# Gates by head in row halves, segment sums in float32r, the gelu eviction ahead of the mix and the norm total on VectorE, in a one-core hybrid decoder layer

## The reference, cut to what matters

```
def rg_lru(x, h0, gate_a_w, gate_a_b, gate_x_w, gate_x_b, lam):
    xb = xf.reshape(B, L, LRU_HEADS, LRU_BS)                  # 16 heads of 64
    r  = sigmoid(einsum('blhi,hij->blhj', xb, gate_a_w) + gate_a_b)
    ig = sigmoid(einsum('blhi,hij->blhj', xb, gate_x_w) + gate_x_b)
    log_a = -LRU_C * r * softplus(-lam)
    a = exp(log_a)
    u = sqrt(-expm1(2.0 * log_a)) * (ig * xf)
    _, h = associative_scan(_lin_combine, (a, u), axis=1)     # h = a*h + u
lru_out = rmsnorm(h * gelu(lru_y), lru_out_norm)

def ssd_scan(x, dt, A, Bm, Cm, h0):
    Acs = cumsum(dtc * A, axis=2)
    seg = Acs[:, :, :, None] - Acs[:, :, None, :]             # per head, 128 x 128 of a chunk
    Lmat = exp(where(causal, seg, -inf))
    y_diag = einsum('bcijg,bcijge,bcjgep->bcigep', CB, Lmat, xdt)
```

## Time and profile before

| what | value |
|---|---|
| median of 3 runs | 2287.48 us (2287.12 to 2287.72) |
| profiled execution, its own time | 2286.77 us |
| its span, first to last instruction | 2285.0 us |
| busy PE / DVE / POOL / ACT | 99% / 45% / 33% / 20% |
| one slot, in slots 2 to 7 | 40.2 us, of 2285 |
| mean granted PE clock | 0.997 |

### The profile page before, as it was taken

One profiled execution on the slowest core, in us unless ns is written; L12 is line 12 of the kernel. 1 busy time (PEld: TensorE's weight loads), 2 busy tenths in 40 slices (PEclk: granted clock), 3 DMA queues, 4 the chain that ended last, 5 costly groups with the idle time before them and its releaser, 6 DMA issues.

```text
span 2285.0 us, 31977 instructions
## 1 busy us (share of the span) xinstructions
PE 2254.6 (99%) x14337; PEld 2196.3 (96%) x14337; DVE 1021.3 (45%) x795; ACT 450.2 (20%) x561; POOL 758.2 (33%) x420
## 2 busy tenths in 40 slices
PE   8999999999999999999999999999999999999997
PEld 8999999999999999988888999999999999999997
DVE  6422122311233557867778586773231123212336
ACT  4100000000002225454453540120000001000102
POOL 4333333333333223333534642323333333333340
PEclk9999999999999999999999999999999999999999
DMA  4111111111112422310110422111111111111112
GB/s 150 47 47 47 47 47 46 47 47 47 47 42 79 129 75 93 119 46 31 52 40 32 175 75 87 47 47 47 47 47 47 47 47 47 47 47 47 47 56 75
DMA packets 48456, 138.87 MB, mean 61 GB/s; under 512 B 7608, under 2 KB 16312, under 8 KB 48320
## 3 DMA queue, kind: packets, MB, share of 16 engines
q1 hardware_dynamic: 47168, 135.78, 18.8%
q10 hardware_dynamic: 1152, 1.05, 0.1%
HBM read 118.19 MB, written 18.79 MB: 60 GB/s over the span
## 4 chain that ended last, share of the span: by engine, by line
PE 89%; DVE 6%; DVEq 2%; issue 1%; ACT 1%; DMA 1%; SPq 0%; ACTq 0%
PE set L568 82%; PE set L799 2%; DVEq L1321 1%; DVE lru_conv L1187 1%; PE pair L701 1%; PE set L701 1%; PE pair L709 1%; DVEq L1285 0%; DVE xbc L1291 0%; DVE e L1286 0%; PE set L588 0%; DVE power L1324 0%; DVEq L1289 0%; PE set L734 0%; PE set L731 0%
## 5 line engine op out<-in xcount | busy, mean ns | idle before, releaser
L457 POOL TENSOR_SCALAR w_hi<-w_raw 128x1024 fp32r<-128x1024 f32 (+1 forms) x181 | 193.9, 1071 | 1418.6 <-PE set L568 1228.5
L459 POOL TENSOR_TENSOR w_lo<-w_raw,w_hi 128x1024 fp32r<-128x1024 f32 (+1 forms) x181 | 445.2, 2460 | 27.6 <-issue 1.4
L568 PE MATMUL set<-x_lo,w_hi 128*128 128x344 f32 x2112 | 448.7, 321 | 3.5 <-DVE x_lo L1087 3.5
L568 PE MATMUL set<-x_hi,w_hi 128*128 128x344 f32 x2112 | 448.9, 321 | 0.8 <-ACT x_hi L842 0.8
L568 PE MATMUL set<-x_hi,w_lo 128*128 128x344 f32 x2112 | 446.2, 320 | 0.0
L568 PEld LDWEIGHTS set<-x_lo,w_hi 128*128 128x128 f32 x2112 | 357.3, 189 | 4.6 <-DVE x_lo L1087 4.6
L568 PEld LDWEIGHTS set<-x_hi,w_hi 128*128 128x128 f32 x2112 | 355.5, 188 | 1.4 <-issue 0.9
L568 PEld LDWEIGHTS set<-x_hi,w_lo 128*128 128x128 f32 x2112 | 352.0, 188 | 0.0
L1083 DVE TENSOR_TENSOR up<-set,rstd 128x1032 f32<-128x1032 f32 x43 | 53.0, 1233 | 419.8 <-PE set L568 419.8
L568 PE MATMUL set<-u_hi,w_hi 128*128 128x344 f32 x864 | 199.4, 339 | 8.5 <-DVE gelu L1083 5.5
L568 PE MATMUL set<-h_hi,w_hi 128*128 128x344 f32 x948 | 201.3, 321 | 0.8 <-DVE h_lo L1107 0.8
(11 more groups left out here) (252 smaller groups left out, 2601.2 us busy)
## 6 DMA issues: line engine op xcount, KB each, us to landing
w_raw<-in_gate_up SPq DMA_DIRECT2D x87, 512.0 KB, 3.5
w_raw<-in_w_in SPq DMA_DIRECT2D x36, 512.0 KB, 4.2
w_raw<-in_down SPq DMA_DIRECT2D x32, 512.0 KB, 3.5
w_raw<-in_w_out SPq DMA_DIRECT2D x16, 512.0 KB, 3.8
w_raw<-in_down SPq DMA_DIRECT2D x16, 384.0 KB, 3.2
x<-in_xt SPq DMA_DIRECT2D x8, 516.0 KB, 8.0
x_kept<-x SPq DMA_DIRECT2D x8, 516.0 KB, 5.0
mixed<-power SPq DMA_DIRECT2D x8, 516.0 KB, 2.9
```

Of the source, the lines that this page charges most:

```text
L457: pool.tensor_scalar(w_hi[s][:, 0:n], w_raw[s][:, 0:n], 1.0, 0.0, ALU.mult, ALU.add)
L459: pool.tensor_tensor(w_lo[s][:, 0:n], w_raw[s][:, 0:n], w_hi[s][:, 0:n].bitcast(F32), ALU.subtract).then_inc(split, 1)
L568: end = pe.matmul(out[:, c, 0:CH], w[s][:, k * P:(k + 1) * P], x[:, kx, c * CH:(c + 1) * CH], start=(first and n == 0), stop=(last and n = ...
```

## The change

It does the following, all of it in the slots but for two small conversions:

- **Gates.** The weights of a tile were two 128x128 block-diagonal matrices (one for each gate, two heads in each). Now they are one 128x128 array: rows 0 to 63 hold the first head's weights for gates a and x side by side, rows 64 to 127 the second head's, x first. `gate` issues six products with 64 rows of contraction, alternating between the row halves, into `pair` (second head) and `set1` (first head). ACT's sigmoids become four of 64 partitions x 1024 and four of 64x8.
- **Segment sums.** `a_tok` is split into a float32r high and low part (`a_hi`, `a_lo`, in the space of `dtw`); POOL makes one 128x2048 product of the high part and two of 128x1024 of the low part (`segr_lo`, which share memory with `lmat`); PE makes each segment sum as two accumulated float32r products in place of one float32 product.
- **Eviction and mix.** `gelu` and the LRU input share two buffers by parity; DVE evicts ly right behind the scan and mixes after it. The scan's result goes to `decay`, the 9-column copy moves to ACT, ACT's `lru_square` moves from the end of a slot to behind the gates of the next.
- **Norm total.** Tiles 1 to 5 of the LRU norm's total are added on DVE, ahead of `lru_power` (in slots 3 to 7), not on POOL.
- **High part of the lx weights.** ACT copies it (for `c` = 1 to 7), and POOL makes the low part alone.

```
@@ gpsimd
-                pool.wait_ge(landed[s], 16 * (u // 2 + 1))
-                pool.tensor_scalar(w_hi[s][:, 0:n], w_raw[s][:, 0:n], 1.0, 0.0, ALU.mult, ALU.add)
-                pool.drain()
+                if name[0] == "lx" and name[1]:
+                    pool.wait_ge(lx_high, name[1])
+                else:
+                    pool.wait_ge(landed[s], 16 * (u // 2 + 1))
+                    pool.tensor_scalar(w_hi[s][:, 0:n], w_raw[s][:, 0:n], 1.0, 0.0, ALU.mult, ALU.add)
+                    pool.drain()
                 pool.tensor_tensor(w_lo[s][:, 0:n], w_raw[s][:, 0:n], w_hi[s][:, 0:n].bitcast(F32),
                                    ALU.subtract).then_inc(split, 1)
...
             def seg_terms(c):
                 if c:
                     pool.wait_ge(seg_done, 2 * c)
+                    pool.wait_ge(y_done, 2 * c)
...
                 pool.tensor_tensor(segr[:], tri[:].unsqueeze(1).broadcast_to([P, HEADS, QC]),
-                                   a_tok[:, c, :].unsqueeze(2).broadcast_to([P, HEADS, QC]), ALU.mult).then_inc(segr_ready, 1)
+                                   a_hi[:, c, :].bitcast(F32).unsqueeze(2).broadcast_to([P, HEADS, QC]), ALU.mult)
+                for g in range(GROUPS):
+                    mine = a_lo[:, c, g * GH:(g + 1) * GH].bitcast(F32)
+                    pool.tensor_tensor(segr_lo[g][:], tri[:].unsqueeze(1).broadcast_to([P, GH, QC]),
+                                       mine.unsqueeze(2).broadcast_to([P, GH, QC]), ALU.mult).then_inc(segr_ready, 1)
...
-                if c >= 3:
-                    total("lru", c - 2, tl)
@@ tensor
                     for n in range(2):
-                        h = g * GH + 4 * n
-                        end = pe.matmul((set1 if g else pair)[:, n, :], later[:],
-                                        segr[:, h:h + 4, :].rearrange("p h t -> p (h t)"), start=True, stop=True)
+                        for low, part in enumerate((segr[:, g * GH + 4 * n:g * GH + 4 * n + 4, :],
+                                                    segr_lo[g][:, 4 * n:4 * n + 4, :])):
+                            end = pe.matmul((set1 if g else pair)[:, n, :], later_r[:],
+                                            part.rearrange("p h t -> p (h t)"), start=(low == 0), stop=(low == 1))
...
-                    for n in range(2):
-                        pe.matmul(set1[:, 2, n * DEC:(n + 1) * DEC], w[:, n, :], lacc[:, PROMPT:T],
-                                  start=True, stop=True)
-                    for n, out in enumerate((set1, pair)):
-                        for k in range(2):
-                            end = pe.matmul(out[:, k, :], w[:, n, :], lacc[:, k * 512:(k + 1) * 512], start=True, stop=True)
-                        end.then_inc(gate_products, 1)
+                    h0, h1 = slice(0, HD), slice(HD, P)
+                    pe.matmul(set1[:, 2, 0:DEC], w[h0, :], lacc[h0, PROMPT:T], start=True, stop=True).then_inc(gate_small, 1)
+                    for k in range(2):
+                        tokens = slice(k * 512, (k + 1) * 512)
+                        pe.matmul(pair[:, k, :], w[h1, :], lacc[h1, tokens], start=True, stop=True)
+                        end = pe.matmul(set1[:, k, :], w[h0, :], lacc[h0, tokens], start=True, stop=True)
+                    end.then_inc(gate_products, 1)
+                    pe.wait_ge(gate_small, c + 1)
+                    pe.matmul(set1[:, 2, DEC:2 * DEC], w[h1, :], lacc[h1, PROMPT:T],
+                              start=True, stop=True).then_inc(gate_products, 1)
@@ scalar
                 if c:
                     lru_gates(c - 1)
+                    if c > 1:
+                        lru_square(c - 2)
                     lru_decays(c - 1)
...
-                first_tap(XT + c, lraw, lacc)
-                if c:
-                    lru_square(c - 1)
+                first_tap(XT + c, lraw[c % 2], lacc)
+                if c < NCH - 1:
+                    u = U(("lx", c + 1))
+                    act.wait_ge(used, u - 1)
+                    act.wait_ge(landed[u % 2], 16 * (u // 2 + 1))
+                    act.activation(w_hi[u % 2][:], w_raw[u % 2][:], ACT.Copy).then_inc(lx_high, 1)
@@ vector
+                if c >= 3:
+                    lru_total(c - 2)
                 if c:
                     lru_power(c - 1)
                 mask(c, 0)
...
                 if c:
                     lru_scan(c - 1)
-                    dve.wait_ge(mixed_ready, c)
-                else:
-                    dve.wait_ge(state_stored[0], 32)
-                scaled(("ly", c), gelu[:], rstd)
+                dve.wait_ge(tails, XT + c + 1)
+                scaled(("ly", c), gelu[c % 2][:], rstd)
+                if c:
+                    lru_mix(c - 1)
```

More of the change, by code:

```diff
@@ L229, in build @@
         c_dec = [at(f"c_dec{g}", Y + k, [DEC, P]) for g, k in enumerate((6, 10))]
-        segr = at("seg_terms", Y, [HEADS, QC])
+        segr = at("seg_terms", Y, [HEADS, QC], F32R)
+        segr_lo = [at(f"seg_low{g}", Y + 2 + g, [GH, QC], F32R) for g in range(GROUPS)]
         lmat = [at(f"lmat{g}", Y + 2 + g, [GH, QC]) for g in range(GROUPS)]
@@ L237, in build @@
         cb = at("cb", Y + 8, [GROUPS, QC], skip=256)
-        gates = at("gates", Y + 8, [2, P], skip=512)
-        gates2 = at("gates2", Y + 8, [2, P], skip=768)
+        gates = at("gates", Y + 8, [P], skip=512)
+        gates2 = at("gates2", Y + 8, [P], skip=768)
         gate_a, gate_x, decay = (at(n, Y + 9 + k, [T]) for k, n in enumerate(("gate_a", "gate_x", "decay")))
-        lraw, lacc = at("lru_in", Y + 12, [T]), at("lru_conv", Y + 13, [T])
-        gelu, sq, sqn, tl = (at(n, Y + 14 + k, [T]) for k, n in enumerate(("gelu", "power", "square", "total_lru")))
+        lraw = gelu = [at("lru_even", Y + 12, [T]), at("lru_odd", Y + 14, [T])]
+        lacc = at("lru_conv", Y + 13, [T])
+        sq, sqn, tl = (at(n, Y + 15 + k, [T]) for k, n in enumerate(("power", "square", "total_lru")))
         zt, t0, t1 = (at(n, XB + k, [T]) for k, n in enumerate(("silu_z", "total_s0", "total_s1")))
@@ L922, in lru_gates, with sigmoid @@
                 par = pars[:, XT + t, :]
[L923 to L927 removed]
+                h0, h1 = slice(0, HD), slice(HD, P)
+                def sigmoid(to, source, at_rows, bias):
+                    return act.activation(to, source, ACT.Sigmoid, bias=par[at_rows, bias:bias + 1])
+                act.wait_ge(gate_products, 2 * t + 1)
+                sigmoid(halves(gate_a[h0, 0:PROMPT]), set1[h0, 0:2, :], h0, PAR_GA)
+                if t:
+                    act.wait_ge(scanned, t)
+                sigmoid(halves(gate_x[h0, 0:PROMPT]), set1[h1, 0:2, :], h1, PAR_GX)
+                act.wait_ge(gate_products, 2 * t + 2)
+                for to, rows, at_rows, cols, bias in ((gate_a, h0, h0, 0, PAR_GA), (gate_x, h0, h1, 0, PAR_GX),
+                                                      (gate_a, h1, h1, DEC, PAR_GA), (gate_x, h1, h0, DEC, PAR_GX)):
+                    last = sigmoid(to[rows, PROMPT:T], set1[at_rows, 2, cols:cols + DEC], at_rows, bias)
+                last.then_inc(gate_read, 1)
+                for to, at_rows, bias in ((gate_a, h1, PAR_GA), (gate_x, h0, PAR_GX)):
+                    last = sigmoid(halves(to[h1, 0:PROMPT]), pair[at_rows, 0:2, :], at_rows, bias)
+                last.then_inc(gate_read, 1)
             def lru_decays(t):
@@ L944, in lru_finish @@
                 freed(("ly", t))
-                act.activation(gelu[:], gelu[:], ACT.Gelu_apprx_tanh).then_inc(gelu_done, 1)
+                act.activation(gelu[t % 2][:], gelu[t % 2][:], ACT.Gelu_apprx_tanh).then_inc(gelu_done, 1)
             def lru_square(t):
@@ L954, in lru_square @@
                     act.wait_ge(added["lru"], t - 1)
+                act.activation(lru_h[:, t, :], decay[:, PROMPT - 1:T], ACT.Copy)
                 act.activation(sqn[:] if t else tl[:], sq[:], ACT.Square).then_inc(squared["lru"], 1)
@@ L1154, in prepare @@
                         dve.drain()
+                dve.wait_ge(consts, 1)
+                dve.tensor_copy(later_r[:], later[:])
                 dve.wait_ge(dtw_landed, 16)
```

59 lines of the change are left out of this document (35 added, 24 removed).

## The result

The changed kernel takes 2311.1 us (median; 2307.26 to 2314.32), the kernel before 2287.6 on the same chip: 1.0104 times, 95% interval 1.0092 to 1.0117, slower by 1.0%. The forecast was 2290.3 with a range to 2301, so the time lies 10 us outside it. The profiled execution, the fastest of the four, took 2307.26 us for a span of 2305.3, 20.3 longer than the span of 2285.0 before; 2.8 of it were forecast.

A forecast was written before the change was run, and what follows sets the result against it. PE, busy 99% of the span, was taken to bound the kernel. Slots 3 to 6 +6.5, slot 7 +1.2, slot 2 -1.1, slot 1 -2.2, slot 0 -1.6: +2.8 on the median 2287.48 gives 2290.3 us, range 2277 to 2301.

The forecast's parts named there:

- that the clock stays at full: All slots: PE keeps full clock despite five holes of 4 us, so no time was added for them.
- the rival of a falling clock: At `outputs(0)` in five slots: half clock behind PE's holes adds 2.8 each, 14 us, to 2304; chance 0.09.
- The main part of the forecast: The whole kernel: +2.8 us to 2290.3, with PE idle some 4 us ahead of `outputs(0)`; chance 0.50.
- Low products at 1.9: POOL in the slots: each new low product of the segment sums takes 1.9 us, 2.4 kept for the range.
- rival 3: POOL in slots 1 to 7: low products cost 2.4 us each like w_lo, +7 us, to 2297.3; chance 0.19.
- Part A: Steady slot from start of lx to start of `outputs(0)`: 21.1 us instead of 18.3, lost 2.8.
- The order at the port: DVE and POOL share a port, whoever asked first goes first: total, skip product, power product, the last ending at 15.3.
- Rival 1: DVE's power product gets in ahead of POOL's skip product: part A 1.7 us shorter in five slots, 2281.8; chance 0.14.
- Part B: Steady slot from `outputs(0)` to the next lx: 20.7 us through w_lo, scan and eviction, against 21.9; saved 1.2.
- Slots 0 and 1: First two slots: -1.6 us in slot 0 from `seg` and gate less waits, -2.2 in slot 1.
- Slot 7 and the z units: Last slot and behind: +2.8, less 1.3 for the gate and 0.3 at the first z unit, +1.2 us.
- the 17-pass pattern: Gates on PE: as in `widen`, second passes overlap the next product's first, 5 passes of 0.43, 2.1 us.

The follow-up runs named there:

- e2: The changed kernel with DVE's addition to the norm total moved behind the second mask; 2298.1 us, ratio 1.0052.
- e3: The changed kernel with twenty unread float32r products on PE ahead of L745 in slots 2 to 7; 2299.4 us, ratio 1.0055.
- e14: The changed kernel with total behind second mask, turn after set1's sigmoids, z load ahead, lmat[1] exp before root and gelu, lx high part on POOL; 2283.4 us.
- e7: The changed kernel with float32 segment sums, total behind second mask, turn waiting only for set1's sigmoids, z load ahead of the store; 2276.8 us.
- e1: The changed kernel with segment sums in float32 again, without low products on POOL; 2288.0 us, ratio 1.0009.
- e13: The changed kernel with ACT's exp of lmat[1] ahead of root and gelu, and DVE's gate product with the root behind the second mask; 2282.7 us.
- e6: The changed kernel with the load of z unit 3 issued ahead of the store of slot 7's mixed tile; 2304.0 us, ratio 1.0074.
- e11: The kernel before with only the eviction of ly ahead of the mix (and the moves it needs) and the z unit's load first; 2275.4 us.
- e8: The changed kernel with float32 segment sums, gates as before the change, total behind second mask, z load ahead of the store; 2276.3 us.
- e4: The changed kernel with gates as before the change: four products of 128 rows, four sigmoids; 2301.0 us, ratio 1.0065.

## Why the prediction was wrong, step by step

The spans, turn to turn, against the forecast's parts (which were cut at lx, some 5 us earlier):

| stretch | before | after | change | forecast |
|---|---|---|---|---|
| to the turn of slot 0 | 942.7 | 945.4 | +2.8 | 0 |
| slot 0 | 35.7 | 37.7 | +2.0 | -1.6 |
| slot 1 | 40.2 | 39.0 | -1.2 | -2.2 |
| slot 2 | 40.2 | 41.9 | +1.7 | -1.1 |
| slots 3 to 6 | 161.2 | 172.9 | +11.7 | +6.5 |
| last turn to the end | 1065.0 | 1068.3 | +3.3 | +1.2 |
| sum | 2285.0 | 2305.3 | +20.3 | +2.8 |

- **The step that failed: that the clock stays at full, with the rival of a falling clock at a chance of 0.09.** The main part of the forecast said itself that PE would stand idle some 4 us in five slots, and took no price for it. The runs give it: 0.8 to 1.6 us for a stretch of 3.4 us (e2, e3, e14) and 2.7 for the one of 6.8. Filling six of the holes took the ratio from 1.0104 to 1.0055 (e3), 11 us; on the forecast's base that is 2300, just inside its range. Nine stretches were seen in the change, which at these prices make some 9 to 16 of the missing 17.5 us (an estimate: those of the first slots were not filled by themselves). The rival was priced at 2.8 per hole in five slots. The rest is the waits at L702 in slots 0 and 1, slot 2's order and the z unit's load, below. The Trainium skill (TensorE: Matmul & The Clock Gate, Why this matters for your kernels) warns of idle gaps between bursts; here the trace agrees, at 0.50 behind holes of 2.1 to 4.0 us, though not behind every hole of 2.5 (e2).
- **The evidence against it was misread.** The prediction cited "in every slice" at full clock. A slice of the page is 57 us and a stretch 3.4, so the tenths could not show it. The windows of the kernel before do show one, and no hole of more than 0.25 us stands ahead of it, but 54 small products (most of 8 columns) in the two microseconds before:

```profile
840.00:842.00 2.00, 2.00 (x54) 1.98 (x52) 0.61 (x2) 1.47 (x3) 0.00 (x0) 1.00 1.11 260
842.00:846.00 4.00, 4.00 (x18) 4.00 (x17) 3.80 (x4) 1.17 (x2) 0.00 (x0) 0.57 0.62 189
846.00:848.00 2.00, 2.00 (x15) 2.00 (x14) 0.21 (x1) 2.00 (x3) 0.26 (x1) 1.00 0.03 12
```

  The sentence "no row here shows such a fall" was true of the rows read, not of the trace. That stretch has a price as well: between the same two points (first transposes of `xbc`, at 829, and turn of slot 0) e7 takes 112.5 without it and e1, with the same float32 sums, 114.1 with it.
- **Low products at 1.9: right.** Measured 1.89; rival 3 did not happen. What the forecast of this stretch had wrong is the gate product: the sigmoids ended 5.2 behind lx, not 3.7, so the second low product (5.0 to 6.9) went ahead of it and not behind. That cost little, as the power product ended at 15.6 and not at 15.3. Part A, forecast 21.1, measured 21.5.
- **The order at the port.** The forecast had total, skip, power; it came out as: skip, total, power, with the wait on the total. The sum of the three is the same. Rival 1 did not happen. The forecast took the opposite order for slot 2, where no total is added ("the power product goes ahead of the skip product"), and there it failed: DVE asked 0.5 us behind POOL, and the power product was held until 1031.4.

```profile
1028.38 1.91 POOL L545 TENSOR_TENSOR xbc<-xbc,vecs 128x1024 f32<-128x1024 f32 x1
...
1028.92 2.46 DVE L1357 SCALAR_TENSOR_TENSOR power<-power,gate_a 128x1032 f32<-128x1032 f32 x1
```

  A hole of 2.5 at L745 and half clock followed; so slot 2, forecast -1.1, measured +1.7.
- **Part B, forecast 20.7.** With full clock (e3) it is 19.9: the scan behind w_lo takes 2.28, not 3.1, because the small addition takes the hold-up. In the change (slot 3) it is 21.3, as PE itself works at half clock. Slots without the clock: 41.4, forecast 41.8. So the chain was followed rightly where it was looked at.
- **Slots 0 and 1, forecast -3.8, measured +0.8; before slot 0, +2.8.** Here the forecast used round estimates. The low products of chunk 0 hold the port ahead of slot 0 and push the eviction of the second z unit (wait of 2.08 at L702; none with float32 sums, e1). But that wait is not what the +2.8 shows: 2.0 of it lie ahead of the first transposes of `xbc` (828.6 before, 830.7 changed), where e13, the same program up to there, has 828.4, so they are scatter between executions; and from there to slot 0 the change takes only 0.7 more (114.8 against 114.1), since it lacks the half-clock stretch of the kernel before. With one there e13 takes 116.3. In slot 1, eight sigmoids with their table load take 6.9 us, PE is at L702 4.5 behind the start of its lx and waits 2.59. The 1.0 for each was taken from starts of whole-row sigmoids, which overlap by 0.1; the half-row ones don't.
- **Slot 7 and the z units, forecast +1.2, measured +3.3.** SP's queue was not followed: the load of the z unit stands behind the store of the mix, which the change moves last (e6).
- **The gates' overlap** was better than the 17-pass pattern: the four products of 512 columns in row halves took 1.8, near the bound of 1.7 for both halves side by side, where 2.1 was forecast. It is hidden in the change and moved nothing.
- **Right:** 0.23 for a float32r segment product, the eviction ahead of the mix worth about a microsecond per slot (e11), ACT's copy free beside float32 sums (e8, e11), a hole of 4 us ahead of L745 (3.3 to 3.6 in slots 3 to 7).
- **What the prediction didn't ask** was why `outputs(0)` needs the power product at all. It doesn't by its data. It must wait for the exp of `lmat[1]`, because it writes the PSUM set (`set1`) that this exp reads, but only ACT's order puts root and gelu between the two exps. It followed the order as if it were a dependence. That was right for the time of this change, but it is the point that e13 frees.

Not settled: why equal holes of 1.8 to 2.6 us are followed by half clock in one slot or run and not in the next (e2, and the list at the end); only that it is so was seen. What e1 and e4 took off the change does not add up to one price per part, since both also take the hole's clock with them.

## What to carry to other kernels

A forecast hole of PE of 3 us or more (all 28 such holes here had half clock) should have the clock's price in the sum, not among the rivals, and each hole has it separately; look at the clock in windows of a microsecond, not in the page's slices. When a chain over other engines ends just ahead of PE, ask which links are data and which only the order of an engine's queue: moving one exp ahead of two independent operations (and DVE's product with the root behind the second mask) was worth 27 us (e13), more than the change as a whole had cost. PE's savings count only after that.
